# The first shift of an adaLN block: twelve of sixteen column blocks summed by VectorE

## What is computed

```python
def modulate(h, shift, scale):
    return h * (1 + scale) + shift

def adaln(cond, w_mod, b_mod):
    m = jax.nn.silu(cond) @ w_mod + b_mod      # w_mod: 2048 x 6*2048
    return jnp.split(m[:, None, :], 6, axis=-1)

sh1, sc1, g1, sh2, sc2, g2 = adaln(cond, lp["w_mod"], lp["b_mod"])
h = modulate(rms_norm(x, lp["g_attn"]), sh1, sc1)
z = h @ w_in                                    # the combined projection
```

## Time and profile before

| what | us |
|---|---|
| median of three runs | 1691.28 |
| lowest and highest | 1690.28, 1692.29 |
| span of the profiled execution | 1691.8 |
| TensorE busy in it | 1591.9 |
| VectorE busy in it | 690.1 |
| ScalarE busy in it | 263.7 |
| POOL busy in it | 106.1 |

### The profile page before, as it was taken

How to read it: one execution, slowest core, us unless ns; L and a number is a source line. 1 busy time by engine, 2 the same in 40 slices (tenths; PEclk the granted TensorE clock), 3 DMA queues, 4 the chain that set the end, 5 groups by cost and what they waited for, 6 DMA issues and landing times.

```text
span 1691.8 us, 18209 instructions
## 1 busy us (share of the span) xinstructions
PE 1591.9 (94%) x6671; PEld 655.4 (39%) x6716; DVE 690.1 (41%) x1361; ACT 263.7 (16%) x706; POOL 106.1 (6%) x192
## 2 busy tenths in 40 slices
PE   5999999999999999999999998999999999998998
PEld 3455555544434444443332332333233233233332
DVE  3113232113245893344444345345344433544444
ACT  2004221112133000011101101110110111111010
POOL 1022100100020100000000000000000000000000
PEclk9999999999999999999999999999999999999999
DMA  9992643535199765599999999999999999999995
GB/s 394 420 385 120 230 193 119 215 109 213 54 368 410 275 264 221 203 366 426 427 429 428 428 425 428 428 424 428 427 426 428 425 424 427 428 428 423 428 427 237
DMA packets 60526, 581.94 MB, mean 344 GB/s; under 512 B 9129, under 2 KB 10121, under 8 KB 16105
## 3 DMA queue, kind: packets, MB, share of 16 engines
q1 hardware_dynamic: 53120, 557.34, 79.6%
q0 software_dynamic: 6064, 23.22, 3.6%
q10 hardware_dynamic: 1296, 0.77, 0.2%
HBM read 584.06 MB, written 7.05 MB: 349 GB/s over the span
## 4 chain that ended last, share of the span: by engine, by line
PE 68%; DMA 17%; DVE 4%; issue 2%; ACT 1%; SPq 0%; POOL 0%; ACTq 0%
PE bank L1298 24%; DMA ring<-in_w 17%; PE bank L1046 14%; PE bank L1208 7%; PE bank L1025 7%; DVE r L1794 2%; PE bank L920 2%; PE bank L1331 2%; PE bank L1133 2%; PE bank L1257 2%; PE bank L1280 1%; PE bank L1108 1%; PE bank L1194 1%; PE bank L1116 1%; PE bank L1313 1%
## 5 line engine op out<-in xcount | busy, mean ns | idle before, releaser
L1298 PE MATMUL bank<-ring,r 128*64 128x512 f32 x1920 | 469.6, 619 | 45.5 <-DMA ring<-in_w 45.5
L1298 PEld LDWEIGHTS bank<-ring,r 128*64 128x64 f32 x1920 | 129.6, 140 | 303.3 <-issue 303.3
L1046 PE MATMUL bank<-ring,r 128*128 128x384 f32 (+1 forms) x672 | 242.4, 519 | 0.0
L2014 DVE TENSOR_TENSOR bank<-bank,r 128x512 f32<-128x512 f32 x180 | 125.9, 700 | 266.2 <-PE bank L1208 266.2
L1331 PE MATMUL bank<-ring,mod_row 128*64 128x512 f32 x896 | 195.4, 593 | 7.9 <-ACT mod_row L1547 7.9
L1025 PE MATMUL bank<-ring,r 128*128 128x512 f32 x384 | 170.0, 595 | 0.0
L1046 PEld LDWEIGHTS bank<-ring,r 128*128 128x128 f32 x672 | 126.9, 191 | 103.7 <-issue 44.7
L1208 PE MATMUL bank<-r 128*128 128x512 bf16 x495 | 137.6, 382 | 7.2 <-issue 7.2
L2016 DVE TENSOR_TENSOR r<-r,bank 128x512 f32<-128x512 f32 x180 | 123.7, 687 | 6.2
L1331 PEld LDWEIGHTS bank<-ring,mod_row 128*64 128x64 f32 x896 | 75.4, 137 | 118.2 <-issue 107.9
L1208 PEld LDWEIGHTS bank<-r 128*128 128x128 bf16 x540 | 38.0, 97 | 167.4 <-DVE r L2016 97.4
(11 more groups left out here) (281 smaller groups left out, 1238.4 us busy)
## 6 DMA issues: line engine op xcount, KB each, us to landing
ring<-in_w SPq DMA_DIRECT2D x180, 2048.0 KB, 17.8
ring<-in_w_mod SPq DMA_DIRECT2D x64, 1024.0 KB, 11.8
ring<-in_w_first SPq DMA_DIRECT2D x32, 1024.0 KB, 25.9
ring<-in_w SPq DMA_DIRECT2D x19, 1024.0 KB, 9.7
ring<-in_w_o SPq DMA_DIRECT2D x16, 1024.0 KB, 6.2
r<-mod_d POOLq DMA_DIRECT2D x8, 1024.0 KB, 8.0
ring<-in_w_aq SPq DMA_DIRECT2D x8, 768.0 KB, 11.4
ring<-in_w_bq SPq DMA_DIRECT2D x8, 768.0 KB, 13.0
```

What stands on the lines that cost most here:

```text
L1046: mm = pe.matmul(acc[acc_of(a)][:, 0:w], h_t[:, k, t * P:(t + 1) * P], wu[:, j, :], start=(k == 0), stop=(k == KD - 1))
L1298: mm = pe.matmul(ps[64 * c:64 * c + 64, :], xg_t[:, j, 64 * c:64 * c + 64], big_cut(slot_of(u), (8, 512))[:, j % 8, :], start=(j == 0), st ...
L2014: v.tensor_tensor(ps[:, :], ps[:, :], g2b[:, min(t, 1), cols], ALU.mult).then_inc(strip_scaled, 1)
```

## The change

Of SH1, the blocks k = 4 to 15 (`SHIFT_FROM` = 4 on) are no longer computed by TensorE. Their weights are laid out on the host by output column: unit ("shift", k) holds for each of 128 output columns the 2048 weights of that column, on one partition, again 1 MB. VectorE multiplies it with the silu of the condition, which lies spread over all partitions in `cond_all`, and sums along the row, with the bias as the start value (`shift_columns`). For that, the two conditions are loaded again as rows, spread by eight TensorE products with a row of ones (`spread_cond`), and put through Silu by ScalarE. The scale is computed as before, as is the shift of the first four blocks. The modulation of `h_t` moves from VectorE to ScalarE. The ones, the condition rows and the products' output (`junk_s`, bfloat16) lie in `gains`, so POOL's loads of the gains wait for the last column. The order and size of the units on SP's queue stay as they are.

```diff
-        units.extend(("first", g, i, m) for g in FIRST_GROUPS for m in range(4))
+        units.extend(("first", SC1, i, m) for m in range(4))
+        units.extend(("shift", 4 * i + m) if i else ("first", SH1, i, m) for m in range(4))
...
+    out["w_shift"] = w_mod[0][:, SH1 * D + SHIFT_FROM * P:(SH1 + 1) * D].T.reshape(KD - SHIFT_FROM, P, D)
...
+        ones_c, cond_rows = gains[:, 0:P], gains[:, P:P + 1024].rearrange("p (c n) -> p c n", c=2)
+        junk_s = gains[:, 0:D // 2].bitcast(BF16)
...
+            def spread_cond(n0, n1):
+
+                for n in range(n0, n1):
+                    c, q = n // 4, n % 4
+                    mm = pe.matmul(spread_bank[n][:, :], ones_c[32 * q:32 * q + 1, :], cond_rows[32 * q:32 * q + 1, c, :],
+                                   start=True, stop=True)
+                mm.then_inc(spread_full, 1)
...
-            for m in range(4):
-                first_unit(0, 1, m)
+            first_unit(0, 1, 0)
+            first_unit(0, 1, 1)
+            pe.wait_ge(cond_in, 4 * 16)
+            pe.wait_ge(xn_read_a, 6)
+            pe.wait_ge(xn_read_v, 6)
+            spread_cond(0, 6)
+            first_unit(0, 1, 2)
+            pe.wait_ge(modt_ready, scale_count(0))
+            pe.wait_ge(cond_ready, 1)
+            spread_cond(6, 8)
+            first_unit(0, 1, 3)
             first_turn(0, 1)
+            pe.wait_ge(cond_ready, 8)
 
             def next_units(i, part):
 
-                for n in ((0, 1), (2, 3), (4,), (5,), (6,), (7,), (), ())[part]:
-                    first_unit(i, n // 4, n % 4)
-                if part in (3, 6):
-                    first_turn(i, part // 6)
+                if 1 <= part <= 4:
+                    first_unit(i, 0, part - 1)
+                elif part == 5:
+                    first_turn(i, 0)
...
+            e.dma_start(cond_rows[0:P:32, 0, :], ins["c_ctx"].rearrange("(q n) -> q n", q=4)).then_inc(cond_in, 16)
+            e.dma_start(cond_rows[0:P:32, 1, :], ins["c"][0].rearrange("(q n) -> q n", q=4)).then_inc(cond_in, 16)
...
-            e.wait_ge(cond_in, 32)
+            e.wait_ge(cond_in, 4 * 16)
...
+            for n in range(8):
+                c, q = n // 4, n % 4
+                ps = (xn_banks + (first_ps[0], xn_banks[0]))[n]
+                e.wait_ge(spread_full, 1 + n // 6)
+                e.activation(cond_all[:, c, q * 512:(q + 1) * 512], ps[:, :], ACT.Silu).then_inc(cond_ready, 1)
...
+            for k in range(KD):
+                e.wait_ge(modt_ready, column_count(k))
+                for c, cols in enumerate((slice(0, P), slice(P, T))):
+                    last = e.activation(h_t[:, k, cols], h_t[:, k, cols], ACT.Identity, bias=mod_t[:, 1, k, c:c + 1],
+                                        scale=mod_t[:, 0, k, c:c + 1])
+                last.then_inc(h_ready, 1)
...
+            def shift_columns(k):
+
+                m = unit_no[("shift", k)]
+                v.wait_ge(*full_of(m))
...
+                w = ring[:, ring_slot(m), :]
+                for c in range(2):
+                    last = v.tensor_tensor_reduce(junk_s, w, cond_all[:, c, :], 1.0, b_shift[:, k:k + 1], ALU.mult, ALU.add,
+                                                  mod_t[:, 1, k, c:c + 1])
+                    if c == 0:
+                        after(last)
+                last.then_inc(modt_ready, 1)
...
             for i in range(1, 4):
-                for c in range(2):
-                    first_copy(i, c)
-                    first_mod(i, c)
-                hmod(i)
+                first_copy(i, 0)
+                shift_columns(4 * i)
+                first_mod(i, 0)
+                for k in range(4 * i + 1, 4 * i + 4):
+                    shift_columns(k)
...
-            g.wait_ge(modt_full, 7)
+            g.wait_ge(modt_ready, column_count(KD - 1))
             for name, dst in gain_of.items():
                 g.dma_start(dst, ins[name][0].partition_broadcast(P)).then_inc(gains_in, 16)
...
-            g.wait_ge(modt_full, 8)
+            g.wait_ge(modt_full, first_count(3, 0))
             load_row(LATER_GROUPS[0])
```

More of the change, by code:

```diff
@@ L74, with first_count, shift_count, scale_count @@
 FIRST_GROUPS = (SC1, SH1)
+SHIFT_FROM = 4
+def first_count(i, c):
+    return i + 2 if i else c + 1
+def shift_count(k):
+    i, j = k // 4, k % 4
+    return 2 + 5 * (i - 1) + (j + 2 if j else 1)
+def scale_count(i):
+    return 2 + 5 * (i - 1) + 2 if i else 1
+def column_count(k):
+    return max(shift_count(k), scale_count(k // 4)) if k >= SHIFT_FROM else 2
 OUT_ORDER = [(0, 0), (0, 1), (0, 2), (1, 0), (1, 1), (1, 2), (2, 0), (2, 1), (3, 0), (3, 1), (2, 2), (3, 2)]
@@ L307, with by_units @@
         ("state_c_kv", (1, 1, P, KV_RANK)), ("state_c_krope", (1, 1, P, ROPE))]
-def by_units(w_mod, w_in, w_o):
+def by_units(w_mod, b_mod, w_in, w_o):
     out = {}
-    first = w_mod[0].reshape(P, 4, 4, 6, 4, 512)[:, :, :, list(FIRST_GROUPS)]
-    out["w_first"] = first.transpose(3, 4, 1, 0, 2, 5).reshape(2, 4, 4, P, D)
+    first = w_mod[0].reshape(P, 4, 4, 6, 4, 512)
+    out["w_scale"] = first[:, :, :, SC1].transpose(3, 1, 0, 2, 4).reshape(4, 4, P, D)
+    out["w_shift0"] = first[:, :, :, SH1, 0].transpose(1, 0, 2, 3).reshape(4, P, D)
+    out["w_shift"] = w_mod[0][:, SH1 * D + SHIFT_FROM * P:(SH1 + 1) * D].T.reshape(KD - SHIFT_FROM, P, D)
+    out["b_shift"] = b_mod[0][SH1 * D:(SH1 + 1) * D].reshape(KD, P).T
     rows = w_in[0].reshape(4, 4, P, -1)
@@ L602, in build @@
         lg_taken = sem("lg_taken")
-        cols_in, brow_full, brow_ready, bias_full, bias_ready, wr_scaled = (sem(n) for n in (
-            "cols_in", "brow_full", "brow_ready", "bias_full", "bias_ready", "wr_scaled"))
+        cols_in, brow_full, brow_ready, spread_full, bias_ready, wr_scaled = (sem(n) for n in (
+            "cols_in", "brow_full", "brow_ready", "spread_full", "bias_ready", "wr_scaled"))
         xa_ready, shift_cols_in, ge_done, first_at, pick_full, rank_taken = (sem(n) for n in (
@@ L639, in unit_source @@
                 _, g, i, m = u
-                return ins["w_first"][FIRST_GROUPS.index(g), i, m].rearrange("p (q n) -> p q n", q=4), (4, 512)
+                w = ins["w_scale"][i, m] if g == SC1 else ins["w_shift0"][m]
+                return w.rearrange("p (q n) -> p q n", q=4), (4, 512)
+            if kind == "shift":
+                return ins["w_shift"][u[1] - SHIFT_FROM], (D,)
             if kind == "in":
@@ L675, in build @@
                 for c, g in enumerate(FIRST_GROUPS):
+                    if c and i:
+                        frees[unit_no[("shift", 4 * i + m)]] = (modt_ready, shift_count(4 * i + m))
+                        continue
                     u = unit_no[("first", g, i, m)]
                     if m == 3:
-                        frees[u] = (first_full, 2 * i + c + 1)
+                        frees[u] = (first_full, first_count(i, c))
                     else:
@@ L681, in build @@
         uses = [0] * SLOTS
-        for u in range(unit_no[("first", FIRST_GROUPS[1], 3, 3)] + 1):
+        for u in range(unit_no[("shift", KD - 1)] + 1):
             if u not in frees:
@@ L775, in _ @@
                 sp.dma_start(cut(slot, shape), src).then_inc(slot_full[slot], 16)
-                if u[0:2] == ("first", FIRST_GROUPS[1]) and u[3] == 3:
-                    i = u[2]
+                if u == ("first", SH1, 0, 3) or u[0] == "shift" and u[1] % 4 == 3:
+                    i = u[1] // 4 if u[0] == "shift" else 0
                     for c, name in enumerate(EARLY):
@@ L1601, in _ @@
             v.memset(csil[:, :, 2:3], 0.0)
+            v.memset(ones_c, 1.0)
             v.memset(first_ps[0][:, :], 0.0)
@@ L1633, in first_mod @@
                                            op0=ALU.add, op1=ALU.mult).then_inc(modt_ready, 1)
[L1635 to L1641, removed]
+            def shift_columns(k):
+                m = unit_no[("shift", k)]
+                v.wait_ge(*full_of(m))
+                if k == SHIFT_FROM:
+                    v.wait_ge(cond_ready, 8)
+                else:
+                    v.wait_ge(modt_ready, shift_count(k - 1))
+                w = ring[:, ring_slot(m), :]
[5 more added lines that the diff above has]
+                last.then_inc(modt_ready, 1)
             scale_xn(0)
@@ L1728, in spread_bias @@
             def spread_bias():
-                v.wait_ge(bias_full, 1)
+                v.wait_ge(spread_full, 3)
                 for c in range(2):
@@ L2137, in _ @@
             for c, row in enumerate(FIRST_GROUPS):
-                g.dma_start(first_rows[c][0:2, :], b_rows[row].partition_broadcast(2)).then_inc(first_rows_in, 16)
+                n_cols = first_rows[c].shape[-1]
+                g.dma_start(first_rows[c][0:2, :], b_rows[row, 0:n_cols].partition_broadcast(2)).then_inc(first_rows_in, 16)
             g.dma_start(first_rows[0][2:3, :], ins["g_attn"]).then_inc(first_rows_in, 16)
+            g.dma_start(b_shift, ins["b_shift"]).then_inc(first_rows_in, 16)
```

(2 more changed lines are left out.)

30 lines of the change are left out of this document (16 added, 14 removed).

## The result

| | runs | median us | lowest and highest us |
|---|---|---|---|
| before, same session | 4 | 1691.78 | 1690.28, 1693.61 |
| changed | 4 | 1703.81 | 1699.93, 1706.88 |

The changed kernel is slower: the ratio of the times is 1.0065, with a 95% interval of 1.0052 to 1.0077, some 11 us; the two medians of the table are 12.0 apart. The predicted time was 1697.9, the range 1691.0 to 1704.5. The execution that was profiled is the quickest of the four (span 1698.1 us, time 1699.93); the other three took 4 to 7 us more, and this spread needs a reason of its own. The one profiled of the kernel before (span 1691.8) is the longest of its four, 1693.61, since the time is 1.8 us above the span in both kernels. So the two profiles lie only 6.3 us apart.

What follows compares the result with a forecast made beforehand. TensorE bounds the kernel, so its first transpose behind the early loop decides: 4.6 us later behind late gain loads, plus 2.0 for the clock, +6.6 on the 1691.8 span, 1698.4; median 1697.9, range 1691.0 to 1704.5.

Steps and rivals of the forecast that it cites:

- Spreading the conditions: Ahead of TensorE's early loop: eight products of 512 columns at 0.86 us each, 6.9 in all, lower bound 0.26 each.
- The columns: VectorE's 12 column sums, two instructions over 2048 columns each: 4.65 us a column, bounds 4.3 and 5.0.
- rival C: VectorE's column sums run at half rate: 9.3 us a column, transpose at 188, +60, 1752 us; chance 0.10.
- The missed wait: TensorE's early loop: nobody waits long in the first three periods; only the i = 3 early weights hold TensorE, until 107.6.
- the forecast's own period: TensorE's early loop: four k take 19.8 us instead of 25.1, the last period 14.4.
- T0: Start of TensorE's early loop in the changed kernel: 41.8 us, bounds 37 and 44; before, 36.51.
- The last column: VectorE sums the last four columns from 96.8, after the k = 12 landing at 96.7, and ends at 115.8 us.
- Modulation: Moved from VectorE to ScalarE: two activations, about 0.7 us with hand-over; k = 15 is modulated at 116.5 without holding TensorE.
- The gain loads: POOL's loads wait for the last column; the tenth, issued 4.9 us behind the first, lands 11.1 later, at 131.9.
- Rival A: POOL's gain loads land soon, in 5.3 us like the first ones: 1690.5 to 1693, no change; chance 0.18.
- The sum: First transpose 4.6 us later, at 132.75, plus 2.0 for the clock: +6.6 on the 1691.8 span, 1698.4; median 1697.9.
- rival D: Later loop start: products with one weight row at the 0.50 clock take 13.8 us instead of 6.9: 1703.5; chance 0.06.

## Why the prediction was right, and where it was not

The mechanism was right: the gain loads became the last thing that the first norm waits for, TensorE stood ahead of the first transpose, a low clock followed, and the delay was passed on one for one until 372 us at least. Two of the signs that the prediction named for being wrong came true all the same, products of one weight row of 0.33 us and TensorE waiting for line 877's operands in the first three periods (1.79 us at 84.01), and neither changed the mechanism. Step by step:

- **Spreading the conditions.** Forecast 0.86 us a product. TensorE's timeline of the changed kernel (the profile shows each product as two records):

```profile
31.04 1.99 PE L901 MATMUL bank<-gains 1*128 1x512 f32 x12
...
39.71 6.00 PE L925 MATMUL bank<-r 128*128 128x320 f32 x12 [1.45 <-ACT r L1467]
```

  Six products in 1.99 us, 0.33 each: nearly the lower bound of 0.26. (Rows 8 give 0.90 for a full product, not 0.86.) The four rows of weights lie on different quarters of the partitions; that this is what lets them overlap is likely, but no run puts them on the same quarter. The loop starts at 39.71 instead of 41.8. But its first twelve records take 6.00 us, not 3.8, with a clock of 0.50 from 38 to 44, so the 2.1 us won were given back; before had the like, a part of 3.05 instead of 1.64 us, and the forecast had not carried it over to the new start.
- **The columns.** Forecast 4.65, measured 4.90 (k = 5 starts at 61.00, k = 6 at 65.90), within the bounds. The sum runs at full rate: 2.35 us for 2048 columns with two float32 operands, as line 1794 without a sum. The quarter microsecond more is reading out the two sums (0.08 each) and the steps between. The Trainium skill, Vector Engine (DVE) Microarchitecture Reference, section Points that are easy to get wrong, has half throughput for the shape with an accumulator and two such sources; this instruction at least doesn't show it, and rival C fell with it.
- **The missed wait.** The forecast took the landing of the early weights of i = 3 from the earlier trace rows, but had TensorE run freely through i = 2. The early weights of i = 2 landed at 84.0 (issued at 60.0 and 62.0, 22.0 us each), while by the forecast's own period TensorE would have asked for them at T0 + 39.6 = 81.4. The wait was 1.8 us in one execution and 3.5 in another, where it brought the low clock and 3 us. This is the term that the sum left out. The median is 5.9 us above the forecast; about half of that goes by this wait, since the early weights sooner took 3.0 off the median.
- **The last column.** Forecast 115.8, measured 117.7: 1.35 because the four columns began at 98.15, behind the scale row that TensorE finished at 97.4 (late by the wait at 84), and not with the landing at 96.7, and 0.5 from the column's price.
- **Modulation.** Two activations take 0.98 us, not 0.7, and TensorE waits for them at the start of the loop (1.45 us at 39.71), for 0.28 us at 62.21 and at the end, where the forecast had no wait for k = 15 (0.50 us at 118.75).
- **The gain loads.** 4.83 us to issue and 11.4 to land, forecast 4.9 and 11.1. Rival A, soon landing, fell: with SP's queue full, the tenth of ten loads needed as long as before. The Trainium skill, DMA: Bandwidth & Descriptors, section Anatomy of one DMA, has about 2 us fixed. By that, as an estimate, POOL's first power, done at 127.6, would have been the last, and the stand some 6 us. The row shows 12.53.
- **The sum.** Transpose forecast 132.75, measured 135.10; loop end 122.0, measured 122.57; clock +2.0, measured +2.3. That makes +9.25 where +6.6 was forecast, and +13.5 in the second profiled execution. The profiled span of 1698.1 next to the forecast's 1698.4 is luck: the 1.7 us that before lost at 380, and about 1.2 further on, cover the difference. There is luck in the range too. The median of 1703.8 lies above the forecast's own bounds (1694.7 to 1702), and inside the range only because its upper end was set by rival D, and D did not happen: its products were to take 13.8 us, and the eight took 3.1.

What stays open: single executions of one kernel differ by up to 7 us. One part is the clock behind the wait at 84 (shown above). Another part sits in short low stretches at places that the change doesn't touch, such as before's at 380 to 382, or the step from +11.5 to +14.5 around 726 us in the second profiled execution of the changed kernel. What sends the clock down in one execution and not in the next was not found. On what the landing of the gain loads depends was not varied either: shown is only that the tenth needed 10.6 to 12.5 us in every kernel, wherever it was issued.

## What to carry to other kernels

Whoever puts scratch data into a tile must look at who loads into that tile next: here the reuse of `gains` alone cost 14 us of a change that wins 3 without it, and 6 with the early weights sooner. Follow a load by its landing and not by its issue, and check every group of a loop against the landings, not only the last, once the loop becomes quicker. A wait of a few microseconds costs more than its length, because the products behind it may run at half the clock (12.57 us here where 10.49 is the price); so a gain ahead of a load that doesn't come sooner can end as a loss.

## What the runs showed of the hardware

- Products with one row of weights and one of data, laid on four different quarters of the partitions in turn, overlap: six of 512 columns in 1.99 us, where one of 128 rows takes 0.9.
- The length of the last pause alone doesn't tell whether the clock falls. At full clock it stayed after 1.79 us (at 84) and 3.29 us (at 107); it was low behind 3.50 us (at 84), 4.90 and 12.53 us, and also behind 2.68 us that followed a row of fillers. At the start of the loop it was at 0.50 from 38 to 44 in the changed kernel's first profile, though no pause between 25 and 44 us was longer than 1.45 us. The low stretch can begin when TensorE works again (0.62 from 136 to 138), and it cost 1.7 to 3 us each time.
- A multiply with a sum over 2048 columns from two float32 operands costs 2.35 us, no more than the multiply and add without a sum.
- The ten small gain loads through POOL's queue, beside a full queue of SP, landed 5.6 us after their issue at the quickest and 11.4 at the slowest, the tenth, in the changed kernel; 5.1 and 12.5 over all kernels here.
